# Moving the small table loads of a two-block transformer kernel from SP's queue to ACT's

## What is computed

```python
for i in range(DEPTH):
    mod = silu_c @ ada_w[i] + ada_b[i]
    h = rms_norm(x, norm_mix_g[i]) * (1.0 + sc1) + sh1
    y = diff_attention(h, ..., t5_bias, lambda_init)   # i == 0
    x = x + g1 * y
    h = rms_norm(x, norm_ffn_g[i]) * (1.0 + sc2) + sh2
    x = x + g2 * grouped_moe(h, router_w, router_bias, ...)
```

## Time and profile before

| | |
|---|---|
| runs | 1686.2, 1692.4, 1696.04 us |
| median | 1692.4 us |
| profiled execution | 1686.49 us |
| its span, first to last instruction | 1684.7 us |
| instructions | 20875 |
| TensorE busy | 1576.5 us (94%), mean granted clock 0.972 |
| VectorE, ScalarE, GpSimd busy | 469.0, 370.1, 37.4 us |
| read from memory | 533.44 MB, 317 GB/s over the span |

### The profile page before, as it was taken

The page is one execution under the profiler, slowest core; times in us unless marked ns, Lnnn a source line. Parts: engine busy times, 40 slices in busy tenths (PEclk is TensorE's granted clock), DMA queues, the critical chain, the costliest instruction groups (busy, mean ns, idle before and its releaser), DMA issues.

```text
span 1684.7 us, 20875 instructions
## 1 busy us (share of the span) xinstructions
PE 1576.5 (94%) x8542; PEld 900.4 (53%) x8542; DVE 469.0 (28%) x1090; ACT 370.1 (22%) x777; POOL 37.4 (2%) x44
## 2 busy tenths in 40 slices
PE   5999879999989999899999998878799999999998
PEld 3664564544465746554444876546554444545444
DVE  2043341222220342422222264432322121212222
ACT  2132231111121332511111342342311111111111
POOL 0000000000000000000000034000000000000000
PEclk9999979999999999899999999989799999999999
DMA  9996648999998676599999400420299999999995
GB/s 324 386 387 241 236 212 352 429 428 429 427 375 311 240 264 257 215 428 429 429 428 416 156 0 1 174 126 0 100 415 428 428 429 429 428 428 429 429 429 235
DMA packets 94673, 535.18 MB, mean 318 GB/s; under 512 B 7935, under 2 KB 11737, under 8 KB 69922
## 3 DMA queue, kind: packets, MB, share of 16 engines
q1 hardware_dynamic: 94258, 534.41, 78.0%
q10 hardware_dynamic: 368, 0.12, 0.0%
HBM read 533.44 MB, written 1.06 MB: 317 GB/s over the span
## 4 chain that ended last, share of the span: by engine, by line
PE 86%; DVE 4%; DMA 4%; SPq 2%; ACT 2%; issue 1%; DVEq 0%; ACTq 0%
PE pair L900 26%; PE bank L889 7%; PE pair L907 6%; PE bank L907 6%; PE bank L634 6%; PE pair L976 4%; PE bank L641 3%; PE bank L950 3%; PE bank L595 3%; PE pair L950 3%; DMA ring<-in_w_dram 3%; PE bank L728 2%; SPq L402 1%; DMA ring<-in_a_w_qkv_dram 1%; SPq L461 1%
## 5 line engine op out<-in xcount | busy, mean ns | idle before, releaser
L900 PE MATMUL pair<-ring,arena 128*64 128x512 f32 x2048 | 447.1, 594 | 3.3 <-DVE arena L2043 2.9
L900 PEld LDWEIGHTS pair<-ring,arena 128*64 128x64 f32 x2048 | 144.7, 137 | 287.8 <-issue 287.8
L889 PE MATMUL bank<-arena 128*128 128x128 f32 x1120 | 140.0, 280 | 10.0 <-DVE arena L2031 10.0
L2056 DVE TENSOR_TENSOR arena<-sq,pair 128x512 f32<-128x512 f32 x32 | 34.0, 1061 | 407.8 <-PE pair L900 407.8
L889 PEld LDWEIGHTS bank<-arena 128*128 128x128 f32 x1120 | 134.1, 197 | 10.6 <-issue 10.6
L634 PE MATMUL bank<-hh,ring 128*128 128x256 f32 x512 | 119.8, 392 | 6.5 <-ACT hh L1355 3.5
L907 PE MATMUL pair<-ring,arena 128*64 128x512 f32 x512 | 116.9, 598 | 0.0
L907 PE MATMUL bank<-ring,arena 128*64 128x512 f32 x512 | 115.3, 592 | 0.0
L634 PEld LDWEIGHTS bank<-hh,ring 128*128 128x128 f32 x512 | 98.9, 196 | 27.4 <-issue 11.5
L1525 ACT ACTIVATE sq<-pair 128x512 f32<-128x512 f32 x32 | 19.1, 597 | 370.5 <-PE pair L900 370.5
L2064 DVE COPY arena<-bank 128x512 f32<-128x512 f32 x32 | 22.1, 692 | 202.7 <-PE bank L907 202.7
(11 more groups left out here) (352 smaller groups left out, 1581.2 us busy)
## 6 DMA issues: line engine op xcount, KB each, us to landing
ring<-in_w_dram SPq DMA_DIRECT2D x96, 2048.0 KB, 15.4
ring<-in_moe_w_gate_dram SPq DMA_DIRECT2D x32, 2048.0 KB, 12.0
ring<-in_moe_w_up_dram SPq DMA_DIRECT2D x32, 2048.0 KB, 16.1
ring<-in_moe_w_down_dram SPq DMA_DIRECT2D x32, 2048.0 KB, 13.8
ring<-in_ada_w_dram SPq DMA_DIRECT2D x24, 2048.0 KB, 17.6
ring<-in_w_mod_dram SPq DMA_DIRECT2D x12, 2048.0 KB, 12.2
ring<-in_a_w_qkv_dram SPq DMA_DIRECT2D x6, 2048.0 KB, 19.0
ring<-in_b_w_qkv_dram SPq DMA_DIRECT2D x6, 2048.0 KB, 12.0
```

Source lines behind the costliest of these rows:

```text
L889: last = mm(b[part][:, cols(k % 4)], h_tok[:, t, cols(k)], pick[:, t, :], start=(t == 0), stop=(t == TT - 1))
L900: last = mm(b[2 + m][half(a), :], x_sel[:, k, half(a)], R8[moe_slot(l, a, m)][:, k, :], start=(k == 0), stop=(k == KT - 1))
L2056: tt(hid.rearrange("p (f q) -> p q f", f=FT), by_row(gate_act), by_row(b[3]), ALU.mult).then_inc(M["hid_ready"], 1)
```

## The change

The issue of the loads in `const_loads` is taken out of SP's stream, where it stood between chunks 4 and 5, and put into ACT's, behind `mods_copy(0)` and ahead of the first layer. The loads, their order and their semaphore stay the same, and so does the wait of TensorE.

```diff
             for n in range(5):
                 load(n)
-            for dst, src in const_loads:
-                sp.dma_start(dst, src, allow_slow_non_contiguous=True).then_inc(const_in, 16)
             for n in range(5, 10):
                 load(n)
             sp.wait_ge(t5_row, turn(t5_row))
...
             act.wait_ge(x_ready, 4)
             norm_root(xT[:, :, :])
             mods_copy(0)
+            for dst, src in const_loads:
+                act.dma_start(dst, src, allow_slow_non_contiguous=True).then_inc(const_in, 16)
             for l in range(2):
                 if l == 1:
                     norm(xT[:, :, :], 0, mod[:, l, SH1:SH1 + KT])
```

## The result

The changed kernel takes 1696.09 us in the median of 20 runs (1691.16 to 1702.61), the kernel before 1689.01 us in the median of 20 (1686.2 to 1696.04). The three runs known before had put it at 1692.4, at the high side of its spread. The ratio is 1.0043, with a 95% interval of 1.0032 to 1.0054: 7.3 us slower (5.4 to 9.1), within the 0.5% called "same" in the prediction, and on the slow side.

A forecast was written before the change was run, and what follows sets the result against it. TensorE was taken to set the pace after the opening, carrying its losses to the end. Landing +5.4, chunk 7's wait -0.9 and clock +0.9 gave +5.4 us on 1692.4: 1697.8 us, range 1689 to 1706.

The forecast's parts named there:

- What bounds the kernel: Whole run: TensorE sets the pace after the opening, so its opening loss or gain carries one for one to the end.
- Removed issues: SP's queue in the opening: without nine table issues, chunk 5 is issued at 21.4 instead of 38.5, without a gap.
- chunk 7's wait of 0.9 us: TensorE before projection 4: chunk 7 is in by 54.4, so its wait goes, -0.9 us.
- Turn about: Engines shared by SP's and ACT's queues: one packet of each in turn, a pair taking 0.095 us.
- The row from 7 to 8.5: Profile before, ACT's vector loads meeting SP's: 184 SP and 173 ACT packets, read as a full queue taking turns.
- the one from 5.5 to 7: Profile before, same two queues: 140 against 64 packets, read as perhaps a queue with little in it.
- The rival with lots of 16: Queues on the engines: served in lots, last table lands at 66.0, +14.1 us, 1706.5 us; chance 0.22.
- The landing of the last table, +5.4 us: TensorE's t5 matmul (line 754): waits for all nine tables, starting at 58.1 instead of 52.66, +5.4 us.
- The hold of ACT, 2.8 us, inside the landing: ACT's projection copies: issues return only at 47.7, stalling TensorE 2.8 us before projection 2, inside the table wait.
- The clock, +0.9 us: TensorE's granted clock after the remaining table wait: a drop costing between 0 and 1.7 us, taken as +0.9 us.
- Early tables: Rival at line 754: tables in before 53.6, only chunk 7's 0.9 us won, 1691.5 us; chance 0.14.
- The sign given for lots: Line 754 in the profile after: starting at 61 or later would show that queues change in lots.

The follow-up runs named there:

- the two sets: The changed kernel measured twice against the kernel before: 1696.09 us, ratio 1.0043, and again 1696.33 us beside 1687.91, ratio 1.0056.
- the form with two tables: Against the kernel before, only two t5 tables ahead, other seven loads behind chunk 13: two on ACT 1688.03 us (0.9993), two on SP 1686.83 us (0.9982).
- the first experiment: Changed kernel, but TensorE's wait before the t5 matmul covers only the two t5 tables: 1697.69 us beside 1688.54, ratio 1.0057; repeated 1696.27 us, 1.0042.

## Why the prediction was right, and which terms were mis-sized

**What bounds the kernel.** Right: TensorE's loss in the opening, 8.85 us, is 8.3 at 985 us, 8.4 in the span, and 7.3 and 8.4 in the medians of the two sets. No wait for transfers in the experts took it up. "One for one" is too strong for a gain of 1 or 2 us, though: clock drops later in the run moved single executions by more, as the form with two tables showed.

**Removed issues.** Right. SP's chunk 5 is issued at 21.57, the trough in the rate is gone, and chunk 7's wait of 0.9 us with it. The bias is not late either: SP's read of it is issued at 67.03, before at 68.97.

**Turn about.** Right, and sharper than the forecast could say: one packet each, down to windows of 0.1 us. The row from 7 to 8.5 was the one to go by; the one from 5.5 to 7 was a queue with little in it. By the rule of the Trainium skill, page "DMA: Bandwidth & Descriptors", section "Queues, rings and completion order", an engine drains a whole packet, typically 9 to 17 descriptors, from one ring before it switches. The counts in windows of 0.1 us disagree, as far as the profile's packets are the descriptors that the page means. The rival with lots of 16 needed 336 chunk packets beside 231 small ones; the counts of 1008 to 1008 and 850 to 852 exclude it, and its 1706.5 us did not come.

**The landing of the last table, +5.4 us.** Mis-sized: it was +9.8 (62.48 against 52.66). The step that failed is "the first small packet is served at 35.9", with its silent addition that from then on the queue is always full. The first issue began at 34.08, as good as on time, but its first packet was served after 37.6, some 3.5 us later beside a full queue, where I had taken 2 us from a landing of 2.5 us measured without chunk packets. And until 41 only 16 of the 54 turns I had counted were taken; why turn about sets in only near 40.5 stays open. 215 packets were left at 41; at 16 x 5 / 820 = 0.098 us (54 to 59 had 820 of SP's packets) they end at 62.0.

**The hold of ACT, 2.8 us, inside the landing.** Right in kind, and in the room of the queue: from 34 to 51.12, when the last issue returned, 1968 small packets were served, 123 per engine, where I had 124. It came at 51.12 and not at 47.7 because these turns began late. The stall was 5.97 us in place of 2.8, and the clock drop behind it, which I had called covered, lengthened projections 2 and 3 by 1.8 us. Together they end only 1.9 us before the landing, so the stall lay inside it, but barely: the first experiment took the landing away and won 2.3 us in the opening.

**The clock, +0.9 us.** It was 0 here: the drop of the long stall was covered, and 1.91 us of wait brought none. With 2.87 us of wait it came, at the 1.7 us stated.

The sum at projection 4 was 9.8 - 0.9 + 0 = 8.9 us, against 5.4 - 0.9 + 0.9. The landing was 4.4 us too low and the clock 0.9 too high; the first carries the miss.

**The total.** That 1697.8 us comes so near to 1696.09 is in part luck. The base of 1692.4 was 3.4 us above the median of 20 runs, and the change of 5.4 us was 1.7 below the difference of the medians, 7.1. The two errors have opposite signs.

**The rivals.** Early tables: excluded by the counts. Changing in lots: the same. The sign given for lots, line 754 at 61 or later, was a bad one: turn about alone, begun late, put it at 62.48, and only the packet counts tell the two apart. The threshold of 61.2 for passing 0.5% was passed too, while the runs' ratio is 1.0043 in one set, below that border, and 1.0056 in the other, above it. The forecast's border between "same" and "slower" was as near as the chances said.

## What to carry to other kernels

When a small load is moved to a second issuing queue, count its packets, not its bytes. From ACT's queue each contiguous run was one, and beside SP's full queue each waited for one packet of 2 KB, here 0.095 us per 16 runs. Look also at how many are outstanding: the last of 231 per engine was taken in only when 123 had been served, and until then ACT stood still. Look then at who waits behind the engine that issues, and whether the wait is for the loads needed now or for all that share a semaphore. Loads with many short runs cost nothing measurable here where the bulk queue waits anyway, in the bulk queue's own order.

## What the runs showed that was not expected

- The strictness of the turns: 850 packets of 2048 bytes against 852 of 16 bytes. The small ones were half of the packets and 0.01 of 1.75 MB.
- The nine loads are 3696 packets from ACT's queue and 304 from GpSimd's, and the second are not cheap: 219 GB/s from 41 to 45.
- The small loads did not start in turn: no packet for 3.5 us after the first issue, and equal counts only from about 40.5. This made most of the miss.
- ACT's issue of one table took 6.14 us and the next 5.99 us, and with SP held back 1.28 and 0.60. The length of an issue shows what is in the queue ahead, not what the load costs.
